# Fox attention of the second block: one unit of two heads and one row block at a time, or a chunk of two heads with both row blocks

## The reference, cut to what matters

```python
def forgetting_block(q_blk, blk, k, v, dcum):
    causal = s[None, :] <= t[:, None]
    d_t = lax.dynamic_slice_in_dim(dcum, blk * Q_BLOCK, Q_BLOCK, axis=2)
    logits = (jnp.einsum('bhqd,bhkd->bhqk', q_blk, k).astype(jnp.float32) * FOX_DIM ** -0.5
              + d_t[..., :, None] - dcum[..., None, :])
    w = jax.nn.softmax(jnp.where(causal, logits, -jnp.inf), axis=-1)
    return jnp.einsum('bhqk,bhkd->bhqd', w.astype(v.dtype), v)

def mixer_fox(x, w_in, b_f, w_out):
    h = x @ w_in
    qkv, f_logit = jnp.split(h, [3 * FOX_HEADS * FOX_DIM], axis=-1)
    q, k, v = qkv.reshape(b, s, 3, FOX_HEADS, FOX_DIM).transpose(2, 0, 3, 1, 4)
    log_f = jax.nn.log_sigmoid((f_logit + b_f).astype(jnp.float32))
    dcum = lax.cumsum(log_f, axis=1).transpose(0, 2, 1)
    o = sweep_query_blocks(lambda qb, i: forgetting_block(qb, i, k, v, dcum), q)
    return o @ w_out
```

## Time and profile before

| | |
|---|---|
| median of the runs | 1299.59 us |
| the profiled execution: own time; span of its trace | 1301.13 us; 1299.3 us |
| mean granted TensorE clock | 0.934 of full |
| busy: PE; DVE; ACT; POOL | 1163.6 us (90%); 754.8 (58%); 546.4 (42%); 0.2 |
| chain that ended last | PE 71%; DVE 16%; ACT 6%; DMA 4%; issue 2% |
| DMA | 200.95 MB, mean 155 GB/s |

### The profile page before, as it was taken

One profiled execution on the slowest core, in us unless ns is written; L12 is line 12 of the kernel. 1 busy time (PEld: TensorE's weight loads), 2 busy tenths in 40 slices (PEclk: granted clock), 3 DMA queues, 4 the chain that ended last, 5 costly groups with the idle time before them and its releaser, 6 DMA issues.

```text
span 1299.3 us, 18592 instructions
## 1 busy us (share of the span) xinstructions
PE 1163.6 (90%) x7908; PEld 1045.8 (80%) x7908; DVE 754.8 (58%) x932; ACT 546.4 (42%) x755; POOL 0.2 (0%) x4
## 2 busy tenths in 40 slices
PE   4879989779999989947879999987999979999997
PEld 2879778559998879946679998886987659999887
DVE  2565556756775455366575665486344457566557
ACT  4562227244443334384543333344444444333333
POOL 0000000000000000000000000000000000000000
PEclk7788999888999998978999999998998979999999
DMA  9522764123555535410235555535431115455551
GB/s 387 229 83 98 287 229 177 61 90 132 193 180 185 193 128 215 150 66 33 98 118 176 194 176 184 193 130 211 147 114 68 63 67 183 175 193 177 192 182 34
DMA packets 33698, 200.95 MB, mean 155 GB/s; under 512 B 3152, under 2 KB 4688, under 8 KB 11984
## 3 DMA queue, kind: packets, MB, share of 16 engines
q1 hardware_dynamic: 32048, 190.30, 40.3%
q10 hardware_dynamic: 1568, 9.46, 1.9%
HBM read 198.70 MB, written 1.05 MB: 154 GB/s over the span
## 4 chain that ended last, share of the span: by engine, by line
PE 71%; DVE 16%; ACT 6%; DMA 4%; issue 2%; ACTq 0%; SPq 0%; DVEq 0%
PE bank L582 21%; PE bank L587 20%; PE bank L588 20%; DMA raw<-wstream 4%; DVE w_lo L1514 4%; PE bank L771 2%; DVE hT_lo L1532 2%; ACT w_hi L1122 1%; PE bank L1030 1%; DVE hT_hi L1531 1%; PE bank L764 1%; PE bank L1029 1%; PE bank L657 1%; PE bank L706 1%; PE bank L674 1%
## 5 line engine op out<-in xcount | busy, mean ns | idle before, releaser
L1514 DVE TENSOR_TENSOR w_lo<-raw,w_hi 128x2048 fp32r<-128x2048 f32 (+1 forms) x159 | 358.2, 2257 | 191.6 <-ACT w_hi L1122 184.5
L1122 ACT ACTIVATE w_hi<-raw 128x2048 fp32r<-128x2048 f32 (+1 forms) x159 | 299.4, 1885 | 280.0 <-PE bank L582 237.7
L582 PE MATMUL bank<-hT_hi,w_hi 128*128 128x256 f32 (+1 forms) x1360 | 392.5, 289 | 20.0 <-DVE w_lo L1514 11.0
L587 PE MATMUL bank<-hT_lo,w_hi 128*128 128x256 f32 (+1 forms) x1360 | 390.0, 287 | 0.0
L588 PE MATMUL bank<-hT_hi,w_lo 128*128 128x256 f32 (+1 forms) x1360 | 389.5, 286 | 0.0
L582 PEld LDWEIGHTS bank<-hT_hi,w_hi 128*128 128x128 f32 (+1 forms) x1360 | 264.9, 195 | 24.5 <-DVE w_lo L1514 12.5
L587 PEld LDWEIGHTS bank<-hT_lo,w_hi 128*128 128x128 f32 (+1 forms) x1360 | 265.1, 195 | 0.1
L588 PEld LDWEIGHTS bank<-hT_hi,w_lo 128*128 128x128 f32 (+1 forms) x1360 | 264.8, 195 | 0.2
L582 PE MATMUL bank<-w_hi,hT_hi 128*128 128x256 f32 (+3 forms) x448 | 148.3, 331 | 32.0 <-DVE w_lo L1514 12.1
L587 PE MATMUL bank<-w_lo,hT_hi 128*128 128x256 f32 (+3 forms) x448 | 144.3, 322 | 0.0
L588 PE MATMUL bank<-w_hi,hT_lo 128*128 128x256 f32 (+3 forms) x448 | 143.7, 321 | 0.0
(11 more groups left out here) (264 smaller groups left out, 1099.4 us busy)
## 6 DMA issues: line engine op xcount, KB each, us to landing
raw<-wstream SPq DMA_DIRECT2D x179, 1024.0 KB, 4.8
arena<-prow ACTq DMA_DIRECT2D x2, 2560.0 KB, 10.4
x_res<-x ACTq DMA_DIRECT2D x1, 1024.0 KB, 14.5
rows<-prow ACTq DMA_DIRECT2D x2, 512.0 KB, 24.0
out<-x_res SPq DMA_DIRECT2D x4, 256.0 KB, 2.1
const_sb<-const ACTq DMA_DIRECT2D x1, 872.0 KB, 18.6
raw<-wstream SPq DMA_DIRECT2D x1, 768.0 KB, 4.1
raw<-wstream SPq DMA_DIRECT2D x1, 544.0 KB, 3.8
```

Source lines behind the costliest of these rows:

```text
L582: ins = mm(o, a[0], b[0], start=start, stop=False)
L587: mm(o, a[0], b[1], start=False, stop=False)
L1122: A(w_hi[n % HI][:, 0:m], raw[:, slot % RAW, 0:m], ACT.Copy).then_inc(weights_rounded, 1)
L1514: V.tensor_tensor(w_lo[slot][:, 0:m], raw[:, slot, 0:m], w_hi[n % HI][:, 0:m].bitcast(F32), ALU.subtract).then_inc(weights_split, 1)
```

## The change

- **Chunks.** Instead of 16 units there are eight chunks. Chunk c is heads 2c and 2c + 1 with both row blocks: 2 x 256 and 2 x 128 logits in two banks, one for each head. Head 2c sits in partitions 0 to 63 of queries and keys, head 2c + 1 in 64 to 127. The four products of queries and keys alternate between the two heads, and so do the four output products, which write partitions 0 to 63 and 64 to 127 of one bank.
- **Decay.** The running sum is split in a high and a low part of fp32r in 16 partitions, with the first 128 columns repeated behind the 256 (decay_hi, decay_lo, 384 columns). Two fp32r products for each head, with 16 rows, replace the fp32 ones.
- **Normalisation.** VectorE multiplies by the reciprocal (fox_normalise) instead of ScalarE.
- **Order of tiles.** fq0.0, fk0.0, fq0.1, fk0.1, fv0.0, fv0.1 and the same for the second eight heads; the pieces of the chunks (L logits, T transposes, O outputs) stand behind tiles by the table FOX_BEHIND, the last ones behind row tiles (FOX_ROWS).
- VectorE copies one 128 x 256 output a chunk, and ScalarE two transposed blocks of 384 columns.

```diff
+FOX_TILES = [("fq0", 0), ("fk0", 0), ("fq0", 1), ("fk0", 1), ("fv0", 0), ("fv0", 1),
+             ("fq1", 0), ("fk1", 0), ("fq1", 1), ("fk1", 1), ("fv1", 0), ("fv1", 1)]
...
-            names += ["ff"] + halves("fq0", "fk0", "fv0", "fq1", "fk1", "fv1")
+            names += ["ff"] + [f"{n}.{j}" for n, j in FOX_TILES]
...
+FOX_BEHIND = {("fq0", 1): ["fd", ("L", 0)], ("fk0", 1): [("L", 1)], ("fv0", 0): [("L", 2), ("T", 0)],
+              ("fv0", 1): [("O", 0), ("T", 1), ("L", 3)], ("fq1", 0): [("O", 1), ("T", 2)],
+              ("fk1", 0): [("O", 2), ("T", 3)], ("fq1", 1): [("O", 3), ("L", 4)], ("fk1", 1): [("L", 5)],
+              ("fv1", 0): [("T", 4), ("L", 6)], ("fv1", 1): [("T", 5), ("O", 4), ("L", 7)]}
+FOX_ROWS = [(0, [("O", 5), ("T", 6)]), (1, [("O", 6), ("T", 7)]), (2, [("O", 7)])]
...
-                        mm(o, negsel[:, h:h + 1].to_broadcast([P, P]), dT[:, 0:K], start=True, stop=False)
-                        return mm(o, qT_c[r:r + 64, c + t * P:c + (t + 1) * P], kT_c[r:r + 64, c:c + K],
-                                  start=False, stop=True)
...
+                    def fox_logits(c):
...
+                        pe.wait_ge(decay_split, 1)
+                        banks = [begin("fox", "L", c, hh) for hh in range(2)]
+                        for part in (decay_hi, decay_lo):
+                            for hh in range(2):
+                                h = 2 * c + hh
+                                mm(banks[hh][:, 0:384], minus_head[0:16, h:h + 1].to_broadcast([16, P]),
+                                   part[0:16, :], start=part is decay_hi, stop=False)
+                        for t, at_ in ((1, 0), (0, 256)):
+                            for hh in range(2):
+                                r, q = 64 * hh, c * T + t * P
+                                last = mm(banks[hh][:, at_:at_ + (t + 1) * P], qT_c[r:r + 64, q:q + P],
+                                          kT_c[r:r + 64, c * T:c * T + (t + 1) * P], start=False, stop=t == 0)
...
+                    def fox_transposes(c):
+
+                        pe.wait_ge(fox_probs_ready, c + 1)
...
+                    def fox_outputs(c):
...
+                        for m, at_ in ((0, 0), (1, P)):
+                            for hh in range(2):
+                                v = m * D + (2 * c + hh) * 64
+                                last = mm(b[64 * hh:64 * hh + 64, at_:T], v_c[:, v:v + 64],
+                                          pT_[:, hh * 384 + m * T:hh * 384 + m * P + T],
+                                          start=m == 0, stop=m == 1)
...
-                    V.memset(dT, 0.0)
+                    V.memset(decay, 0.0)
+                    V.tensor_copy(minus_head[:, :], const[:, CONST["negsel"]:CONST["negsel"] + 16])
...
-                    lo_ahead("fv0.1")
+                    link(V.tensor_copy(decay[0:16, T:T + P], decay[0:16, 0:P]))
+                    link(V.tensor_copy(decay_hi[0:16, :], decay[0:16, :]))
+                    V.tensor_tensor(decay_lo[0:16, :], decay[0:16, :], decay_hi[0:16, :].bitcast(F32),
+                                    ALU.subtract).then_inc(decay_split, 1)
...
+                    def fox_normalise(c):
+
+                        p_, m = fox_probs[c % 3], 4 * (c % 2)
+                        dve.wait_ge(fox_exp_done, c + 1)
+                        link(V.reciprocal(rinv[:, m:m + 4], rowsum[:, m:m + 4]))
+                        for at_, K in ((0, T), (512, P)):
+                            for hh in range(2):
+                                L = p_[:, at_ + hh * K:at_ + (hh + 1) * K]
+                                last = V.tensor_scalar(L, L, rinv[:, m:m + 1], None, ALU.mult)
+                                m += 1
+                        last.then_inc(fox_probs_ready, 1)
...
+                    lo_ahead("fk0.0")
                     b = wait_full("fd")
                     done(V.tensor_copy(dtok.rearrange("p (t h) -> p t h", t=2),
                                        b[:, 0:T].rearrange("p (t n) -> p t n", t=2)[:, :, 0:16]), "fd")
...
+                    lo_ahead("fq0.1")
+                    fox_logits(0)
+                    lo_ahead("fk0.1")
+                    fox_logits(1)
+                    lo_ahead("fv0.0")
+                    fox_normalise(0)
+                    fox_logits(2)
...
+                    fox_logits(5)
+                    lo_ahead("fv1.0")
+                    fox_normalise(4)
+                    fox_logits(6)
+                    lo_ahead("fv1.1")
+                    fox_normalise(5)
+                    dve.wait_ge(psum_full, full("fv1", 1))
+                    split_mixed(0)
+                    fox_output(4)
+                    fox_logits(7)
+                    split_mixed(1)
+                    lo_ahead("o1_0.0")
+                    fox_normalise(6)
```

More of the change, by code:

```diff
@@ L154, with fox_keys @@
 ROW_TILES = {row_name(stage, pair): (stage, pair) for stage in ROW_STAGES for pair in range(4)}
-FOX_UPPER = [("fq1", 0), ("fq1", 1), ("fk1", 0), ("fk1", 1), ("fv1", 0), ("fv1", 1)]
-def fox_order():
-    order = []
-    for i in range(19):
-        order += [("fox", what, i - late) for what, late in (("L", 0), ("T", 2), ("O", 3)) if 0 <= i - late < 16]
-        if 1 <= i <= 6:
-            order.append(FOX_UPPER[i - 1])
-        order += [("rows", pair, half) for step, pair, half in FOX_ROWS if step == i]
-    return order
+FOX_BEHIND = {("fq0", 1): ["fd", ("L", 0)], ("fk0", 1): [("L", 1)], ("fv0", 0): [("L", 2), ("T", 0)],
[3 rows of a table added]
+FOX_ROWS = [(0, [("O", 5), ("T", 6)]), (1, [("O", 6), ("T", 7)]), (2, [("O", 7)])]
+def fox_keys(what, c):
+    return [("fox", what, c)] if what == "O" else [("fox", what, c, hh) for hh in range(2)]
 def stick_order(n):
@@ L273, in psum_plan @@
             plan.append(("ff",))
-            for n in ["fq0", "fk0", "fv0"]:
-                gemm(n)
-            plan.append(("fd",))
-            order = fox_order()
-            first = order.index(("fox", "L", 8))
-            plan.extend(order[:first])
+            for n in FOX_TILES:
+                plan.append(n)
+                for piece in FOX_BEHIND.get(n, ()):
+                    plan.extend([("fd",)] if piece == "fd" else fox_keys(*piece))
+            first = plan.index(("fox", "T", 5, 0))
+            behind = plan[first:]
+            del plan[first:]
             within(range(BANKS))
-            beside_rows("o1", order[first:])
+            beside_rows("o1", behind + [key for _, pieces in FOX_ROWS for piece in pieces for key in fox_keys(*piece)])
         transposes(f"ln1_{layer}")
@@ L450, in build @@
         qT_c, kT_c, v_c = cut(2048), cut(2048), cut(2048)
-        dT, dtok = cut(256), cut(32)
+        dtok = cut(32)
         f_y, f_l = cut(256), cut(256)
+        decay_hi, decay_lo = rounded("decay_hi", 384, top[0]), rounded("decay_lo", 384, top[0] + 384)
+        minus_head = rounded("minus_head", 16, top[0] + 768)
+        top[0] += 784
+        decay = cut(384)
+        fox_probs = [cut(768) for _ in range(3)]
+        fox_probsT = [cut(768) for _ in range(2)]
+        assert top[0] <= lay_at
         csil = tiny[:, 0:8]
@@ L744, in attention @@
                         continue
-                    if key in FOX_UPPER:
-                        half = token_half if key[0] == "fv1" else feature_half
-                        half(f"{key[0]}.{key[1]}", **({"n": T} if key[0] == "fv1" else {}), key=key)
-                        continue
                     _, what, i = key
-                    if (name, what, i) == ("fox", "L", 8):
-                        for upper in FOX_UPPER:
-                            in_sbuf(*upper)
                     g, par, t = us[i]
@@ L1035, in _ @@
+                    for pair, pieces in FOX_ROWS:
+                        row_half("o1", pair, 0)
+                        row_half("o1", pair, 1)
+                        for piece in pieces:
+                            fox_piece(piece)
                 row_half(f"o{layer}", ROW_STAGES[f"o{layer}"][3], None)
@@ new lines, in fox_transposed @@
+                    def fox_transposed(c):
+                        for hh in range(2):
+                            b = wait_full("fox", "T", c, hh)
+                            if c >= 2:
+                                act.wait_ge(psum_full, full("fox", "O", c - 2))
+                            done(A(fox_probsT[c % 2][:, hh * 384:(hh + 1) * 384], b[:, 0:384], ACT.Copy),
+                                 "fox", "T", c, hh)
+                    fox_input("fq0", 0)
+                    fox_input("fk0", 0)
@@ new lines, in _ @@
+                    fox_input("fq0", 1)
+                    fox_exp(0)
+                    fox_input("fk0", 1)
+                    fox_exp(1)
+                    fox_input("fv0", 0)
+                    fox_transposed(0)
+                    fox_exp(2)
+                    fox_input("fv0", 1)
+                    fox_transposed(1)
+                    fox_exp(3)
+                    fox_input("fq1", 0)
```

(3 more changed lines are left out.)

161 lines of the change are left out of this document (112 added, 49 removed).

## The result

| | before | after |
|---|---|---|
| median of the runs compared, us | 1299.57 (1299.45 to 1299.69) | 1263.24 (1262.47 to 1264.07) |
| ratio after / before, 95% interval | | 0.9724 [0.9708, 0.9739] |
| profiled execution, us (span) | 1301.13 (1299.3) | 1262.67 (1260.9) |
| mean granted clock | 0.934 | 0.937 |
| Fox stage, start of fq0.0 to the end of the last row tile, us | 167.4 | 129.7 |

The changed kernel is faster by 36.3 us, 2.8%; the forecast was 1266.5 us, with 33.8 us saved by its sum. The profiled spans differ by 38.4 us, of which the stage holds 37.8. The stage starts 1.1 us earlier (893.9 against 895.0), which is within what executions of one kernel differ by there; behind it the two traces agree to half a microsecond (236.9 us before, 237.3 after).

A forecast was written before the change was run, and what follows sets the result against it. TensorE was taken to bound the Fox stage. Savings of 24.1 us in streaming, 2.5 in waits and 7.2 in half clock, 33.8 in all, gave 1265.8 us, stated as 1266.5 with an allowance for overlap; range 1257 to 1280.

The forecast's parts named there:

- decay products, a chunk: Logits on TensorE: 32 fp32r products of 384 columns in 16 rows, 0.183 us each, 0.73 us a chunk.
- head products: Query-key products of two heads run side by side on array halves: 0.70 us a chunk, bounds 0.65 and 1.30.
- changes of shape in the logits: Three changes of array shape in a chunk's logits at 0.14 us each: 0.42 us.
- transposes: Six transposes a chunk in one group instead of two: 0.80 us against 0.95.
- outputs: Eight output records a chunk on two column halves: 0.85 us against 1.60, bounds 0.80 and 1.45.
- waits: TensorE's waits in the Fox stage fall from 10.3 to 7.8 us, saving 2.5 us.
- half clock costs: Stretches at 1.2 GHz in the Fox stage cost 6.4 us instead of 13.6, saving 7.2; bounds 3.0 and 13.6.
- Halves one after the other: Head and output products don't run side by side: 0.60 us more twice a chunk, 9.6 us, 1276; chance 0.12.
- VectorE's chain at each transpose: VectorE's chain ends last, so every transpose waits: 11 us more plus 10 at half clock, 1287; chance 0.12.
- The 16-row product in more than one pass: The 16-row fp32r decay product isn't single-pass and costs 0.65 us: 15 us more, 1281; chance 0.05.
- A clock that falls behind each burst: Each of 13 bursts is followed by 6.8 us at half clock: 41 us more, 1307; chance 0.03.
- Nothing visible: The whole change shows no visible effect on the kernel's time; chance 0.02.

The follow-up runs named there:

- the run with fp32 decay: Changed kernel with one fp32 decay product of 128 rows and 384 columns per head instead of two 16-row fp32r ones: 1266.63 us, ratio 0.9775.
- The early splits: Changed kernel with VectorE splitting fk0.0 before waiting for the forget gate and fk0.1 before waiting for the transposed decay: 1255.40 us, ratio 0.9684.
- the one-shape unit of the kernel before: Kernel before, with decay products of even heads cut to 64 rows, the head products' shape: 1294.17 us, ratio 0.9981; a 256-key unit took 1.93 us against 2.40.
- the other order: Changed kernel with two tiles split earlier, plus normalisations of chunks 4, 5 and 6 ahead of the next tile's split: 1254.86 us, ratio 0.9676.
- the repeat: The changed kernel run again unaltered, compared with the kernel before on the same chip: 1263.41 us, ratio 0.9751.
- the two runs on one half: Changed kernel with both heads' head products reading partitions 0 to 63 (1266.31 us, ratio 0.9764), or both outputs written there (1266.61 us, 0.977).
- the decay between: Changed kernel with the second pair of decay products moved between the head products of 256 and of 128 columns: 1264.65 us, ratio 0.9754.

## Why the prediction was right

The forecast of 1266.5 us stands 3.3 above the median, inside the range, and its likeliest case is the one that happened. It is no luck of errors that cancel: all three terms of the sum came out too small, streaming by 2.0 us, waits by 0.5 and half clock by 3.0, against 0.9 for a term it lacked. Point by point, for the stage:

| term | forecast, us | measured, us |
|---|---|---|
| decay products, a chunk | 0.73 | 0.71 (records 0.18 apart) |
| head products | 0.70 | 0.65 |
| changes of shape in the logits | 0.42 | 0.38 |
| transposes | 0.80 | 0.63 in five chunks, 0.81 in three |
| outputs | 0.85 | 0.80 |
| eight chunks save | 24.1 | 52.1 - 26.0 = 26.1 |
| waits | 7.8, save 2.5 | 4.3 + 0.4 + 0.8 + 1.8 = 7.3, save 3.0 |
| half clock costs | 6.4, saves 7.2 | 3.0, saves 10.2 |
| sum | 33.8 | 39.3 |

The 26.0 are 8 x 1.75 + 5 x 0.63 + 3 x 0.81 + 8 x 0.80. Half clock is counted as half of TensorE's busy time in such stretches: 26.5 / 2 = 13.2 before, 6.00 / 2 = 3.0 after. From the 39.3 go 0.9, a term that the forecast didn't have: ten tiles are now followed by products of another shape, and the last record of such a tile holds 0.09 us longer (5.94 us in place of the 5.85 of the run with fp32 decay). That gives 38.4 against 37.8 measured, 0.6 left over; counting half a stretch's busy time as lost is rough, and the early splits put the 3.0 at 2.6. In the medians 36.3 arrived; the rest is what the part ahead of the stage does in one execution or another.

**Streaming.** The steps that were read from rows held: the rate by columns for a 16-row record (0.183 forecast, 0.177 measured), the excess by alternation (confirmed from both sides, by the one-shape unit of the kernel before and the extra changes put into the kernel after) and its size. I had put it at 0.14 for each of five changes. That was a miscount: a unit's four products alternate 128, 64, 128, 64 rows, three changes, and the exit is a fourth, of which only the first half falls inside. The records show 0.19 for each of 3.5, with some 0.1 on either side of a change, which is the same 0.67. Three of my changes in a chunk are 0.38 for the same reason: the entry from a tile has only its second half. The choice between factors of overlap went too far toward L828: with two halves it is 2.0, and the 0.05 that I put on in both places aren't there. For transposes I added 0.15 for changes; where a tile follows, their exit costs nothing.
The Trainium skill (TensorE: Matmul & The Clock Gate, Measured speedup vs the span model) gives for a pack of tiles the time of one plus some 4 ns for each further one. The trace agrees in size: partners start 6 ns apart where the partner stands two records later in the program, 13 ns where it stands four later. Its factors of 3.07 and 2.38 for four and three tiles, which I had used for a counter-estimate, would have made two halves too dear: 0.84 against the 0.65 measured, sixteen times, 3.0 us in all.

**Waits.** All stand where forecast: 3.40 (3.5), 0.87 (0.6), 0.2 twice (0.4), 0.80 (0.8), 1.80 (2.1). The second was too low by 0.27: 0.4 + 0.2 + 2.25 of VectorE stood against 2.25 of TensorE in the forecast, and the logits were 0.1 shorter, the split starts 0.65 behind L1023 (917.17 to 917.82), and TensorE's end of wait lies 0.05 behind its end. The early splits took the first two away and left the others, and the other order took away the two small ones and most of the one at chunk 6.

**Clock.** This is the term that was mis-sized. I counted 1.3 for the first stretch, 3.4 behind one of the small waits and 1.7 at the last row tile. Measured: the first stretch is twice as long (6.8 us) and costs 3.0 counted so, or 2.6 by the run without it, and there is none behind the waits of 0.2 to 0.9. The whole stage has 6.8 us at half clock where I said about 13. At the last row tile a stretch of 3.4 us appears in five of the eleven traces of the changed kernel and its variants (in the repeat from 1017.9) and in the first trace not; so that this part of my 6.4 was missing from the compared trace is chance. That the first stretch comes from the wait of 3.4 us is shown: without the wait there is none from 888 to 1007 us. What removed the three stretches of 6.8 us of the kernel before is not shown part by part. No variant of the changed kernel has one between the first stretch and the last row tile, not even the one in which ScalarE scales, with four waits of 0.6 to 1.3 us; fewer changes of shape alone shortened the first of them to 3.4. So the 10.2 us, the second largest term, are measured, but their causes are argued.

**Rivals.** Halves one after the other (1276): refuted by the pairs of starts and by the two runs on one half, and its price was right, 0.65 and 0.64 in place of the 0.60 I took. VectorE's chain at each transpose (1287): only one wait of 0.8 and two of 0.1 to 0.2; with ScalarE scaling there are three waits of 0.6 to 1.3, the nearest to that rival's picture. The 16-row product in more than one pass (1281): 0.18 us refutes it. A clock that falls behind each burst (1307): between 909.2 and 1023.4 us not one of the bursts was followed by a stretch. "Nothing visible": no.

## What to carry to other kernels

Count changes of the array's shape, not only columns: here each cost 0.19 us, nearly a whole record of 256 fp32 columns (0.216), and putting the records of one shape together (0.99 us a chunk) paid more than a cheaper number format (0.59). The largest part of the saving, 0.65 us a chunk twice, is the halves: two groups on separate halves, of rows or of columns, took half the time, with partners two or four records apart in the program. And when a forecast finds a long wait of the bounding engine, ask at once whether its cause can be issued earlier: moving two splits on VectorE ahead of their waits brought another 7 us in the stage, a fifth of what the whole change did.

## What the runs showed that I had not expected

- A record started ahead of earlier ones of the program when its half was free: with the records by head, all four of 256 columns start ahead of the first of 128, so the fifth began 13 ns behind the first and 0.3 us ahead of the second.
- The cost of a change lies on both sides of it: the last record holds its successor some 0.09 us longer, the first one behind holds its own 0.10. Transposes (fp32) followed by a projection (fp32r), both with 128 rows and columns, cost nothing: the tile's first product starts 28 ns behind the last transpose and the second 0.205 us behind the first, 0.233 for the two, against 0.109 + 0.120 for one of each in a row. Half of a change also hides in the tile ahead of it, so counting the pieces of the chunk alone misses it.
- A wait of 3.4 us was followed by 6.8 us at half clock, where one of 2.3 us in the kernel before was followed by 3.4; those of 0.8 and 0.9 us by none. Why the stretch in some executions at the last row tile comes and goes, for the same kernel, stays open.
- Where the part ahead of the change varies by 1 to 3 us, a distance between two instructions inside the stage repeated to 0.01 us in the two traces of the changed kernel. Three of these experiments (the fp32 product, the decay between, ScalarE scaling) have effects of 2.6 to 3.2 us that the medians don't show apart from the changed kernel.
